# A routing step moved one place forward in a software pipeline, on TensorE and VectorE, and later seeds in the last stage

## The reference

```python
x = x + y @ w_out[l]
h = _rmsnorm(x, norm_mem[l])
memn = _rmsnorm(mem, norm_memkv[l])
x = x + mem_cross_attention(h, memn, w_mq[l], w_mkv[l], w_mo[l])   # 4 heads, 256 memory rows
h = _rmsnorm(x, norm_ffn[l])
x = x + hier_moe(h, w_rg[l], b_rg[l], w_re[l], b_re[l], w_e_gu[l], w_e_dn[l])
return _rmsnorm(x, norm_final)
```

## Time and profile before

| | |
|---|---|
| median of 3 runs (us) | 1234.72 (1234.33 to 1235.63) |
| the profiled execution's own time (us) | 1234.33 |
| its span in the profile (us) | 1232.2 |
| mean granted TensorE clock | 0.978 |
| idle of TensorE before line 2535, the largest group (us) | 8.1 |
| cross-attention pipeline with the router (us from the start) | about 776 to 868 |
| ranks, tables, warm-up (us) | 868 to 891 |
| experts (us) | 891 to 1189 |
| last sum and norm (us) | 1189 to 1232 |

### The profile page before, as it was taken

How to read it: one execution, slowest core, us unless ns; L and a number is a source line. 1 busy time by engine, 2 the same in 40 slices (tenths; PEclk the granted TensorE clock), 3 DMA queues, 4 the chain that set the end, 5 groups by cost and what they waited for, 6 DMA issues and landing times.

```text
span 1232.2 us, 16849 instructions
## 1 busy us (share of the span) xinstructions
PE 1166.2 (95%) x6773; PEld 639.3 (52%) x6773; DVE 552.1 (45%) x1231; ACT 357.0 (29%) x688; POOL 124.1 (10%) x145
## 2 busy tenths in 40 slices
PE   7999999999999899888899999899999999999986
PEld 6445644445744799764554444475733333333332
DVE  6876143243799165875742222254611221212226
ACT  5024711112685231126551111553101111111113
POOL 2100022120000000011100000221111111111000
PEclk9999999999999899899899999999699999999999
DMA  8121121221114432600340004511199999999528
GB/s 274 37 71 35 35 80 60 81 81 59 35 69 172 132 105 55 246 4 1 138 166 6 1 1 142 221 70 52 41 401 427 420 424 421 420 416 416 236 111 317
DMA packets 67267, 199.51 MB, mean 162 GB/s; under 512 B 25612, under 2 KB 42224, under 8 KB 56432
## 3 DMA queue, kind: packets, MB, share of 16 engines
q1 hardware_dynamic: 59328, 181.39, 38.0%
q0 software_dynamic: 7808, 16.96, 3.7%
q10 hardware_dynamic: 48, 0.01, 0.0%
HBM read 172.63 MB, written 35.14 MB: 169 GB/s over the span
## 4 chain that ended last, share of the span: by engine, by line
PE 76%; DVE 10%; ACT 4%; issue 3%; DMA 3%; POOL 0%; DVEq 0%; SPq 0%; POOLq 0%; ACTq 0%
PE bank L2535 20%; PE bank L1528 13%; PE bank L1588 8%; PE bank L1554 7%; PE bank L1647 2%; DMA arena<-y_d 2%; PE bank L1603 2%; PE bank L2662 2%; PE bank L1513 2%; PE bank L1666 1%; PE bank L805 1%; PE bank L916 1%; PE bank L866 1%; PE bank L853 1%; PE bank L884 1%
## 5 line engine op out<-in xcount | busy, mean ns | idle before, releaser
L2535 PE MATMUL bank<-arena 128*128 128x512 f32 (+3 forms) x1032 | 358.1, 507 | 8.1 <-ACT arena L2039 6.8
L2535 PEld LDWEIGHTS bank<-arena 128*128 128x128 f32 x1032 | 197.0, 192 | 163.0 <-issue 140.7
L1528 PE MATMUL bank<-arena 128*32 128x512 f32 x1536 | 169.4, 592 | 1.1 <-DVE arena L1288 1.1
L1528 PEld LDWEIGHTS bank<-arena 128*32 128x32 f32 x1536 | 50.7, 110 | 114.3 <-issue 114.3
L1588 PE MATMUL bank<-arena 128*128 128x512 f32 x220 | 95.6, 592 | 0.0
L1554 PE MATMUL bank<-arena 128*32 128x512 f32 x768 | 87.4, 595 | 0.7 <-ACT arena L1190 0.7
L1297 DVE TENSOR_TENSOR arena<-arena,bank 128x256 f32<-128x256 f32 x25 | 10.5, 422 | 166.1 <-ACT arena L1186 159.5
L2039 ACT ACTIVATE arena<-bank 128x512 f32<-128x512 f32 (+1 forms) x57 | 28.4, 504 | 167.4 <-PE bank L2535 166.9
L1357 DVE TENSOR_TENSOR arena<-arena,bank 128x512 f32<-128x512 f32 x32 | 22.0, 688 | 102.0 <-PE bank L1588 79.5
L1588 PEld LDWEIGHTS bank<-arena 128*128 128x128 f32 x220 | 41.3, 190 | 49.7 <-issue 49.7
L2025 ACT ACTIVATE arena<-arena 128x1024 f32<-128x1024 f32 x26 | 27.4, 1054 | 125.0 <-DVE arena L1357 95.0
(11 more groups left out here) (397 smaller groups left out, 1609.3 us busy)
## 6 DMA issues: line engine op xcount, KB each, us to landing
arena<-in_w_e_gu SPq DMA_DIRECT2D x27, 2048.0 KB, 17.5
arena<-in_w_e_dn SPq DMA_DIRECT2D x33, 1024.0 KB
arena<-in_w_in SPq DMA_DIRECT2D x11, 1024.0 KB
arena<-y_d SPq DMA_DIRECT2D x8, 1024.0 KB, 6.9
arena<-hz_d SPq DMA_DIRECT2D x4, 1792.0 KB, 7.8
arena<-in_w_e_gu SPq DMA_DIRECT2D x6, 1024.0 KB
arena<-in_w_e_gu SPq DMA_DIRECT2D x12, 512.0 KB
pk_d<-arena SPq DMA_DIRECT2D x8, 640.0 KB, 2.9
```

Of the source, the lines that this page charges most:

```text
L1528: ins = mm(bank[part, :], hgT[:, k, part], w_gu(es[i] % NB, k), start=(k == 0), stop=(k == KT - 1))
L2535: ins = mm(psum[PROJ_BANKS[u % 3]][0:rows, 0:n], lhs(k), rhs(k), start=(k == 0), stop=(k == kt - 1))
```

## The change

It has three parts. TensorE's router of a tile is taken from behind the scores of the next turn and put behind the second half of that tile's row transposes; the loop then needs one turn fewer. VectorE's add_out(it-2, 0) is moved from ahead of route to behind it (and, in turn 10, nothing of it is left to move past place_tokens). In the last stage the seeds of tiles 4 to 7 are issued right ahead of their own product instead of three products earlier.

```diff
 dve_tail2:
                 if 0 <= it - 3 < NT:
                     normed_rows(it - 3)
-                if 0 <= it - 2 < NT:
-                    add_out(it - 2, 0)
                 if 0 <= it - 4 < NT:
                     route(it - 4)
                 if it == NT + 2:
                     place_tokens(0)
                 if 0 <= it - 2 < NT:
+                    add_out(it - 2, 0)
                     add_out(it - 2, 1)
 pe_tail2:
-            for it in range(1, NT + 4):
+            for it in range(1, NT + 3):
                 if it + 1 < NT:
                     scores(it + 1)
-                if 0 <= it - 4 < NT:
-                    router(it - 4)
...
                 if 0 <= it - 3 < NT:
                     rows_transposes(it - 3, 1)
+                    router(it - 3)
 pe_tail3:
             for m in range(NT):
+                if m >= 4:
+                    start(m)
                 y_wait(pe, m)
...
-                if 4 <= m + 3 < NT:
-                    start(m + 3)
```

## The result

| | before | changed |
|---|---|---|
| median of 10 runs (us) | 1233.56 (1229.08 to 1235.63) | 1239.46 (1236.37 to 1245.73) |
| ratio | | 1.0054, 95% interval 1.004 to 1.0069 |
| profiled execution (us), its span | 1234.33, 1232.2 | 1238.52, 1236.4 |

The ratio is 6.7 us of 1234, with an interval of 4.9 to 8.5; the two medians differ by 5.9; 7.7 was forecast. All ratios here are made without three slow executions (1731 to 3782 us, one each of e1, e3 and e5) and are not quotients of the medians beside them.

A forecast was written before the change was run, and what follows sets the result against it. TensorE, busy 95% of the span, was taken as the bound. Router 3.0, add 4.6, seeds 0 and 0.1 for gaps made 7.7 us; with 1234.33 and 0.4 for the median, 1242.4 us, 8-in-10 range 1237.5 to 1245.8.

The forecast's parts named there:

- The router behind its own transposes: TensorE's loop: four new waits for ACT's copy (routers 0, 1, 2, 6), 0.76 us each, 3.0 us in all.
- The add behind route in turns 4 to 6: Output product waits 1.18 us per turn for VectorE's add, 3.5 in all; add at S+5.62, S being the start of scores.
- Turn 7: Loop turn without row_max: the add behind route was to cost 0.05 us.
- Turn 8: Loop turn without probability product: the add could start only after route's end, so nothing was to be lost.
- Turn 9: Loop turn whose product already waited 0.44 us for the add: route going first was to add 1.0 us of wait.
- The late seeds: Last stage: transfers on SP's queue set the end, so moving seeds costs 0; bounds nothing gained, 1.7 us lost.
- a changed length of the last stage: Sign of being wrong: the experts or the last stage changing their length; the last stage was expected as long as before.
- The sum: Whole kernel: 3.0 for the router, 4.6 for the add, 0 for seeds, 0.1 for operations not closing up: 7.7 us.
- The clock: Rival: more falls of TensorE's clock in the loop, about 1.7 us each; one more gives 1244.1, two 1245.8; chance 0.20.
- What takes the clock down: TensorE's clock: by the skill's rule the change leaves it alone; the trace shows a fall with no idle above 0.69 nearby.
- faster than before: Rival: TensorE's clock stays at 2.4 GHz where it fell, giving back 4.4 us in sum against 7.7; chance 0.03.
- router's waits alone: Rival: VectorE keeps ahead, so only the router's 3.0 us is lost and nothing for the add, 1237.8 us; chance 0.13.

The follow-up runs named there:

- e1: Kernel before with only the router put directly behind its own transposes, VectorE and last stage as before; ratio 1.0032 (1.0017 to 1.0048).
- e3: Kernel before with only the seeds of tiles 4 to 7 moved right ahead of their products; ratio 0.999 (0.9972 to 1.0008).
- e5: Kernel before, but no output tile stored until the last of eight loads of expert rows has landed; ratio 0.9993 (0.9975 to 1.001).
- e2: Kernel before with only VectorE's first add moved behind route, TensorE as before; ratio 1.0011 (0.9996 to 1.0025).
- e4: Kernel before with the router and add moves together, seeds as before; 1239.74 against 1232.18 us, ratio 1.0063 (1.0044 to 1.0081).
- e6: e4 plus 0.87 us of repeated transposes per turn in turns 4 to 6, ahead of the waiting product; ratio to kernel before 1.0055.
- n1: Kernel before with the router moved later: behind values in turn 7, behind the first output product in turns 8 and 9; ratio 1.0039 (1.0015 to 1.0064).
- n2: n1 plus the late seeds; 1235.85 against 1233.25 us for the kernel before, ratio 1.0019 (1.0 to 1.0038).
- n4: Kernel before plus five unused dense products in TensorE's waits; ratio 0.9973. Its clock reckoning: span times what is missing to granted clock 1.00, mean over executions.
- n5: Kernel before with n4's products except ahead of router 5, values(7) and turn 9's router behind first output products, and late seeds; ratio 0.9974 (0.9963 to 0.9986).

## Why the prediction was right

- **The router behind its own transposes**, forecast 4 x 0.76 = 3.0 us: e1 measured 3.9 (2.1 to 5.9 by its interval), with the four new waits at the places named, 0.69 idle each. Right; the 0.9 above the forecast is within the interval.
- **The add behind route in turns 4 to 6**, forecast 1.18 us each and only together with part 1. In turn 5 of the changed kernel the product came 825.66 - 823.70 - 0.87 = 1.09 us late. The counted points fit too: row_max at S+1.19, normed_rows at S+2.75, route at S+3.42, the add at S+5.53 against S+5.62. e2 has no such wait, e4 has it, and e6 shows that it sets the turn. Right, 0.1 too large each. Turn 6 has the same wait (0.92). In the profiled execution turn 4 had none, since a fall of the clock slowed TensorE by 1.6 us there and hid it; e4's turn 4, at full clock, has it.
- **Turn 7**, forecast 0.05: no wait. The changed kernel had a fall of the clock there that could have hidden one; e4, without a fall in that turn, has none either. **Turn 8**, forecast nothing: 0.51 in place of 0.44. **Turn 9**, forecast 1.0: the product came 865.62 - 863.61 = 2.01 behind the transposes (lines below), before 1.04, so 0.97. From its router to the transposes of tile 7 it took 12.38 us (860.00 to 872.38) against 10.55, where 1.9 more was forecast. Right.

```profile
863.61 0.60 PE L1655 MATMUL bank<-ident,arena 128*128 128x128 f32 x4
865.62 1.95 PE L1646 MATMUL bank<-arena 128*128 128x512 f32 x4 [1.41 <-DVE arena L1357]
```

- **The late seeds**, forecast 0 with 0 to 1.7 lost as bounds. This is the weak step. The prediction took the landing of the last transfer as fixed and named a changed length of the last stage as a sign of being wrong, and that stage came out 3.4 us shorter in the changed kernel's trace (the experts, named with it, were 1.1 longer, which no part of the change explains). The landing is not fixed: from first seed to last product it is 29.9 to 32.7 us in the four traces with late seeds, and 28.6 to 33.3 in those without. e5's trace shows one thing that may move it, the stores issued behind the last load; n1's, quick with those stores, stands against it. Whether late seeds gain is not settled. Three comparisons point the same way, e3 against before 1.0 thousandth, the changed kernel against e4 0.9 and n2 against n1 2, and none is separated from nothing. By what they would gain is open.
- **The sum**, 7.7: e4, which is the sum without seeds, measured 7.8. The changed kernel's 6.7 lies below it by what part 3 may have given.
- **The clock** as a rival: more falls came (two in the loop here and in e1, three in e4, one before), at 1.7 us each, but e3 and e5, whose loops are those of before, also had two. So the traces alone do not tell. The mean of what the clock took, reckoned as under n4, is 28.6 us in the changed kernel, 28.6, 27.8 and 28.5 in e1, e4 and e6, against 26.9 to 27.6 for the kernel before. By this estimate from granted clocks given to 0.001, about 1 to 2 us more went to the clock wherever the router had been moved, which the sum left out. It may explain why e1 lies above its 3.0, and it works against what part 3 may have given. That two terms left out, each about 1 us and of opposite sign, let the sum come within 1 us of the measured ratio is in part luck.
- **What takes the clock down.** The prediction set the trace against the rule of the Trainium skill that it cites ("TensorE: Matmul & The Clock Gate", "Why this matters for your kernels"), that long idle gaps do. The traces stay with this: at 845.7 us the clock fell with no idle above 0.69 us nearby, at 866.2 with none above 0.78, and n4 and n5, with dense products in such waits, had no fall from 833 to 866 us, where each of the eleven other traces had at least one. n4 gained 3.3 us, inside the 4.4 that the rival "faster than before" allowed for a warm clock.

The rival "router's waits alone" is ruled out by e4 against e1, 4.5 us in the medians and 3.8 in the ratios.

## What to carry to other kernels

In a software pipeline, an instruction put directly behind what it depends on shows the whole latency of the engine between (here 0.69 us of ACT's copy); and work taken from ahead of a consumer takes away the time in which another engine was getting ready for it (here the router's 1.9 us, in which VectorE had kept ahead). So count for each engine when its queue reaches the step, from the event that starts the chain, and not how busy it is. Before a step is moved out of a gap, look at every engine's queue that the gap hid, not only at the wait that the step shows.

## What the runs showed of the hardware

- In the kernel before, TensorE's granted clock fell to 1.2 GHz after transposes, a wait of 0.69 us and a router, with no longer idle nearby (845.7 us); after the same sequence at 834.53 it did not. A dense product in each such wait (0.81 us in the timeline) went with 2.4 GHz through turns 7 to 9 in n4 and n5, and with 4.1 us less taken by the clock in the mean of n4's runs. I had taken such falls as chance.
- The last load of 1 MB took 6.8 us with no stores behind it (e5), and 7.5 to 9.0 in eleven traces with finished tiles' stores issued right behind it; in a twelfth of the kind (n1) it took 6.2. What made n1's quick is open.
